# Second block's attention on one core: values of the latents a step later, copies ahead of splits, first sums ahead of a low part, no constant products

## What is computed

```
proj = rms_norm_2(x, attn_norm[l]) @ w_in[l]
h_mla, h_diff, h_ch = jnp.split(proj, [IN_MLA, IN_MLA + IN_DIFF], axis=-1)

# latents (MLA), 6 heads: queries and keys/values come out of small latents
q  = (rms_norm_2(c_q,  q_norm)  @ w_uq)
kv = (rms_norm_2(c_kv, kv_norm) @ w_ukv)
k_nope, v = kv[..., :MLA_NOPE], kv[..., MLA_NOPE:]

# differential, 6 heads, two score maps each; chunk, 4 heads with a relative bias
p = jax.nn.softmax(s, axis=-1)
o = einsum('bhqk,bkhd->bqhd', p, v)

x = x + jnp.concatenate([o_mla, o_diff, o_ch], axis=-1) @ w_out[l]
x = x + conv_ffn_2(rms_norm_2(x, ffn_norm[l]), w_ffn_in[l], ...)
```

## Time and profile before

| | us |
|---|---|
| median of 3 runs (1663.99 to 1665.25) | 1664.72 |
| profiled execution, its own time | 1663.76 |
| its span, from first to last instruction | 1662.5 |
| PE busy in the span | 1604.8 (97%) |
| DVE busy | 1045.5 (63%) |
| ACT busy | 804.7 (48%) |
| POOL busy | 238.1 (14%) |
| share of PE in the chain that ended last | 81% |
| mean granted TensorE clock | 0.993 |

### The profile page before, as it was taken

The page is one execution under the profiler, slowest core; times in us unless marked ns, Lnnn a source line. Parts: engine busy times, 40 slices in busy tenths (PEclk is TensorE's granted clock), DMA queues, the critical chain, the costliest instruction groups (busy, mean ns, idle before and its releaser), DMA issues.

```text
span 1662.5 us, 26953 instructions
## 1 busy us (share of the span) xinstructions
PE 1604.8 (97%) x10878; PEld 1387.7 (83%) x10878; DVE 1045.5 (63%) x1936; ACT 804.7 (48%) x1517; POOL 238.1 (14%) x284
## 2 busy tenths in 40 slices
PE   5999999999999999999999999999999999999998
PEld 3788778877777888887899988878999898799986
DVE  3553856366255435697787667656776667667765
ACT  2332963343233323568455544555555556555553
POOL 1110420011011000012011101132111013221110
PEclk9999999999999999999999999999999999999999
DMA  9557022353554224021445452424555533245552
GB/s 378 215 221 273 18 80 102 147 208 149 205 228 180 99 102 152 3 78 49 177 178 207 179 188 105 153 77 153 177 178 181 190 142 116 103 151 182 184 205 76
DMA packets 39419, 257.28 MB, mean 155 GB/s; under 512 B 5504, under 2 KB 6784, under 8 KB 10496
## 3 DMA queue, kind: packets, MB, share of 16 engines
q1 hardware_dynamic: 36416, 249.61, 41.1%
q0 software_dynamic: 1296, 4.72, 0.8%
q10 hardware_dynamic: 1584, 1.23, 0.3%
HBM read 254.49 MB, written 1.05 MB: 154 GB/s over the span
## 4 chain that ended last, share of the span: by engine, by line
PE 81%; DVE 10%; ACT 5%; DMA 2%; issue 2%; POOL 0%; SPq 0%; DVEq 0%; ACTq 0%
PE ps L485 24%; PE ps L487 24%; PE ps L486 24%; PE ps L501 2%; DVE wl L1758 1%; ACT arena L1665 1%; PE ps L632 1%; ACT wh L1317 1%; PE ps L654 1%; PE ps L641 1%; DVE ps L2017 1%; PE ps L527 1%; DMA arena<-in_xT 1%; PE ps L1066 1%; DMA raw<-in_ev_w_in 1%
## 5 line engine op out<-in xcount | busy, mean ns | idle before, releaser
L1758 DVE TENSOR_TENSOR wl<-raw,wh 128x1024 fp32r<-128x1024 f32 (+2 forms) x324 | 378.3, 1209 | 372.6 <-ACT wh L1317 372.0
L1317 ACT CAST wh<-raw 128x1024 fp32r<-128x1024 f32 (+2 forms) x334 | 328.7, 1034 | 515.7 <-PE ps L487 401.6
L485 PE MATMUL ps<-xh,wh 128*128 128x256 f32 (+1 forms) x1582 | 493.5, 312 | 3.0 <-ACT arena L1622 1.7
L487 PE MATMUL ps<-xh,wl 128*128 128x256 f32 (+1 forms) x1582 | 488.5, 309 | 0.0
L486 PE MATMUL ps<-xl,wh 128*128 128x256 f32 (+1 forms) x1582 | 488.5, 309 | 0.0
L485 PEld LDWEIGHTS ps<-xh,wh 128*128 128x128 f32 x1582 | 301.8, 191 | 28.1 <-issue 10.8
L486 PEld LDWEIGHTS ps<-xl,wh 128*128 128x128 f32 x1582 | 302.0, 191 | 15.2 <-issue 0.7
L487 PEld LDWEIGHTS ps<-xh,wl 128*128 128x128 f32 x1582 | 301.9, 191 | 15.2
L485 PE MATMUL ps<-wh,xh 128*128 128x512 f32 (+3 forms) x812 | 299.5, 369 | 13.9 <-DVE xl L2149 5.6
L487 PE MATMUL ps<-wh,xl 128*128 128x512 f32 (+3 forms) x812 | 294.6, 363 | 0.0
L486 PE MATMUL ps<-wl,xh 128*128 128x512 f32 (+3 forms) x812 | 294.6, 363 | 0.0
(11 more groups left out here) (212 smaller groups left out, 1840.9 us busy)
## 6 DMA issues: line engine op xcount, KB each, us to landing
raw<-in_ada SPq DMA_DIRECT2D x48, 1024.0 KB, 7.3
raw<-in_up SPq DMA_DIRECT2D x44, 1024.0 KB, 5.0
raw<-in_fin SPq DMA_DIRECT2D x44, 1024.0 KB, 4.8
raw<-in_down SPq DMA_DIRECT2D x22, 1024.0 KB, 4.8
raw<-in_fout SPq DMA_DIRECT2D x22, 1024.0 KB, 4.8
raw<-in_win SPq DMA_DIRECT2D x12, 1024.0 KB, 4.9
raw<-in_ev_w_in SPq DMA_DIRECT2D x9, 1024.0 KB, 8.0
raw<-in_wout SPq DMA_DIRECT2D x8, 1024.0 KB, 4.8
```

Of the source, the lines that this page charges most:

```text
L485: e.matmul(out, A[0], B[0], start=first, stop=False)
L487: return e.matmul(out, A[1], B[0], start=False, stop=last)
L1317: e.copy(hi_of(j)[:, a:b], raw_of(j)[:, a:b]).then_inc(*S.hi.up((j, half)))
L1758: e.tensor_tensor(lo_of(j)[:, a:b], raw_of(j)[:, a:b], hi_of(j)[:, a:b].bitcast(F), ALU.subtract).then_inc(*S.lo.up((j, half)))
```

## The change

It is made at eight places, the same in both layers:

1. PE: the two products for the latents' values leave `up_keys` (step 3) and become `up_values`, called in step 4 ahead of `column(7, 0)`. They go to banks 4 and 6 in place of 6 and 7.
2. PE: `keep(7, 2)`, `keep(b, 3)` and `keep(2, 5)` are taken out.
3. PE: `transposes` waits for the normalised probabilities first and for the bank second.
4. ACT and DVE: in step 2 the copies of the latents' queries stand ahead of the split of the `ukv` chunk.
5. ACT and DVE: the copies of the latents' values move from step 3 to step 4, ahead of the split of `win` 8, behind step 4's softmax work.
6. DVE: the low part of `wout` 1 moves from step 10 to step 11.
7. DVE: in step 13 `add_part("d", ...)`, the first sums, stands ahead of `mixed_low(10)`, the last low part.
8. `nb[0] = 0` restarts the turn of banks so that `column(7, 0)` still takes bank 7 and `column(7, 1)` bank 6.

```diff
@@ tensor_program
                     free[b] = [(side[g % 2], ("kn", l, g))]
-                for t, b in enumerate((6, 7)):
+
+            def up_values():
+                j = J[f"ukv{l}", 0]
+                hv, lv = hi_of(j), lo_of(j)
+                for t, b in enumerate((4, 6)):
                     wait_bank(b)
...
             def transposes(i):
                 for m in range(1 if i < 6 else 2):
                     b = 2 + (i % 2 if i < 6 else m)
+                    q.wait_ge(*(S.gps if m else S.vec).at((key, "norm", i)))
                     wait_bank(b)
-                    if i == 10 and m == 0:
-                        keep(b, 3)
-                    q.wait_ge(*(S.gps if m else S.vec).at((key, "norm", i)))
...
                     if i == 4:
-                        keep(7, 2)
+                        up_values()
+                        nb[0] = 0
                     column(7, i - 4)
...
-            keep(2, 5)
             for t in (1, 0):
                 out("m", t, [2], True, False, 1)
@@ scalar_program
             def beside(i):
-                if i == 3:
+                if i == 2:
+                    for g in range(3):
+                        copy2(("uq", l, g), QN[:, g, :], scale=qsc)
+                elif i == 3:
                     copy2(("kn", l, 0), KN[:, 0, :])
                     copy2(("kn", l, 2), KN[:, 2, :])
+                elif i == 4:
                     copy2(("vm", l, 0), VM[:, 0, :])
...
-                elif i == 2:
-                    for g in range(3):
-                        copy2(("uq", l, g), QN[:, g, :], scale=qsc)
@@ vector_program
-                if i == 3:
-                    copy2(("kn", l, 1), KN[:, 1, :])
-                    copy2(("vm", l, 1), VM[:, 1, :])
-                elif i == 10:
-                    turned_low(i)
-                if i in (1, 2, 3, 4, 10):
-                    weights(after({1: J[win, 5], 2: J[win, 6], 3: J[f"uq{l}", 0], 4: J[f"ukv{l}", 0], 10: J[win, 9]}[i]))
-                if i == 1:
-                    copy2(((win, 6), 1), VD[:, 1, :])
-                elif i == 2:
+                if i == 2:
                     q.wait_ge(*S.ea.at(("csq", l)))
...
+                elif i == 3:
+                    copy2(("kn", l, 1), KN[:, 1, :])
+                elif i == 4:
+                    copy2(("vm", l, 1), VM[:, 1, :])
+                elif i == 10:
+                    turned_low(i)
+                if i in (1, 2, 3, 4, 11):
+                    weights(after({1: J[win, 5], 2: J[win, 6], 3: J[f"uq{l}", 0], 4: J[f"ukv{l}", 0], 11: J[win, 9]}[i]))
+                if i == 1:
+                    copy2(((win, 6), 1), VD[:, 1, :])
...
-                if i == 13:
-                    add_part("d", 1)
-                    add_part("d", 0)
...
                 if 0 <= i - 1 < A.n:
                     normalise(i - 1)
+                if i == 13:
+                    add_part("d", 1)
+                    add_part("d", 0)
                 if i > A.lag:
                     mixed_low(i - A.lag - 1)
```

## The result

The changed kernel takes **1652.16 us** (median of 4 runs, 1651.02 to 1652.56); the kernel before took 1664.99 us beside it (4 runs, 1663.99 to 1665.42). The ratio is 0.9924, with an interval from 0.9912 to 0.9936: faster by 12.8 us. The profiled execution is the fastest of these four.

A forecast was written before the change was run, and what follows sets the result against it. It took PE's waits for releasers on DVE and ACT, not the constants, as the bound. Per layer 1.01 + 1.83 + 2.68 - 0.25 = 5.27 us, 10.5 for two, gave 1654.2 us, range 1652.4 to 1658.0.

The forecast's parts named there:

- three signs of being wrong: Pair 10's transposes still wait for DVE; `column(7, 0)` not at least 1 us earlier; a granted clock of 0.50 between them.
- Steps 2 to 4: Early attention loop: DVE's low part of `win` 7 comes 1.39 us earlier, leaving 1.01 us per layer at pair 4's transposes.
- The 0.37 us for the queries: Steps 2 and 3: PE gains 0.82 us from earlier query copies, of which only 0.37 us is left on DVE's chain.
- Steps 5 to 9: Middle of the loop: nothing touched up to step 10, so 1.0 us per layer is carried through.
- Pair 10 and part "m": Steps 10 to 13: pair 10's transposes start 1.83 us earlier, and part "m" gains 2.68 us more, per layer.
- `wout` 0: Behind part "m"'s start: PE waits for DVE's low part of this chunk; 0.25 us charged per layer, bounds 0 and 1.2.
- The sum: Both layers: 1.01 + 1.83 + 2.68 - 0.25 = 5.27 us per layer, 10.5 us in all.
- what a shifted phase may give in later stretches: Stretches after the loop: reason for extending the range's lower end from 1652.9 to 1652.4 us.
- The early part is real: Answers the rival that steps 2 to 4 give nothing, steps 10 to 13 keep 4.26 per layer: 1656.2 us, chance 0.13.
- The clock did not fall: Answers the rival of half-rate falls in the loop: at most 1.7 us each, one per layer gives 1657.6, chance 0.09.
- rival of the cheap constants: Pair 10 and part "m": DVE stays the bound, removed constants only become idle time; 1662 to 1665 us, chance 0.04.
- unseen releaser: Condition of the rival of the cheap constants: another engine's work holds pair 10's transposes and part "m" where they are.

The follow-up runs named there:

- number 1: Kernel before with only the three constant products that the change removes taken out; 1666.82 us beside 1664.40, ratio 1.0026.
- number 4: Changed kernel with `keep(b, 3)` ahead of pair 10's transposes and `keep(2, 5)` behind the loop put back; 1658.26 us beside 1664.22.
- number 2: Kernel before with only the late part of the change (1656.42 us, ratio 0.9954), or only the early part, steps 2 to 5 (1662.28 us, ratio 0.9986).
- number 5: Changed kernel, one edit undone each: splits ahead of queries' copies, 1653.23 us; wait order in `transposes`, 1652.79; low part of `wout` 1 in step 10, 1656.65.
- Numbers 5 and 6: 5 has its line under number 5; 6 is the changed kernel with part d's sums behind the last low part again, 1661.05 us beside 1664.17.
- number 7: Changed kernel with ACT splitting `wout` 0 ahead of its last-values work (1652.22 us, ratio 0.9928), or with `keep(7, 2)` back behind `up_values` (1653.32, 0.9933).

## Why the prediction was right, and where it was not

- **What bounds.** Right. The waits and not the constants set the loop: number 1 shows the constants worth nothing (or less) to remove alone, number 4 that 3.3 of 5.7 us are gone when the late ones stay. None of the three signs of being wrong that the prediction names was seen.
- **Steps 2 to 4.** Right by mechanism and size. 1.37 us was foreseen at the column and 1.51 found, 1.01 at pair 4 and 1.09 found; the waits of 0.6 to 0.8 and about 1.3 us came as 0.62 and 1.04; number 2 has the part alone at 1.11. The 0.37 us for the queries is the 0.4 of number 5.
- **Steps 5 to 9, "nothing from there to step 10 is touched".** The step of the sum that failed. Part 3, the order of the waits, was charged at nothing, without a reason. The gain grows from 1.09 to 1.32 us between pair 4 and pair 9, and by number 5 some 0.19 of these 0.23 us are that order. This is some 0.4 us in both layers, too little to put the time outside the range.
- **Pair 10 and part "m".** Right: 1.84 us for 1.83, 2.74 for 2.68. Numbers 5 and 6 undo one each and lose 1.9 and 2.6 us.
- **`wout` 0.** Right: 0.17 us by the ladder for the 0.25 charged, and 0.12 of it gone in number 7.
- **The sum.** 5.73 us a layer and not 5.27, so 11.4 us and not 10.5: 0.9 of the 2.0 us by which the median differs from the forecast. In a layer 0.23 us of the 0.46 came in steps 5 to 9 (0.15 to 0.19 of them the order of the waits), 0.08 is the early part, 0.06 part "m", 0.01 pair 10, and 0.08 the charge for `wout` 0, which was taken too high. With the measured 11.4 us in place of 10.5, the prediction's own reckoning gives 1653.3, inside its range.
- **The unchanged code, and the range.** This is the step that put the time outside. The prediction took the rest of the kernel over as it was in the median of the runs before (1664.72), and allowed 0.5 us below its best case, "for what a shifted phase may give in later stretches". The measured median is 1.1 us below the 1653.3. In the traces the difference lies ahead of the change and not behind it: 1.3 us of the spans' difference is there where nothing is changed, and the same program's runs span 5.9 us (1662.08 to 1667.94). The median of a new measurement can lie a good microsecond off for that reason alone, as 12.8 and 11.3 us for one and the same change show. Which side of the range's end the first four executions fell on was luck; that the range left no room for it was the mistake.
- **Rivals.** The early part is real (number 2). The clock did not fall in any loop of the changed kernel; numbers 1 and 6 show falls where the waits are longer, and a fall cost 0.8 to 1.5 us there, not more than the prediction's 1.7. Of the rival of the cheap constants one half was seen, that taken out alone they only turn into idle time (number 1); the unseen releaser that it needs is not there, since pair 10 and "m" came earlier once DVE's order had moved.

## What to carry to other kernels

Filler work in front of a wait costs nothing and is worth nothing to remove, until the releaser comes early; then it costs all of its pitch. So price the filler and the releaser's order as one edit: find what the releasing engine does ahead of the work that is waited for, and move that. Compare two executions from a mark just ahead of the changed place, and give the range of a forecast the spread of the unchanged code on either side.

## What the runs showed of the hardware

TensorE's clock fell in this loop only where constants were gone and the order was the old one at that place: behind the wait of 1.44 us in one of two loops (number 1), behind 2.60 us in three of four (numbers 1 and 6), behind 1.75 to 1.82 us in none of four (numbers 1 and 5), behind 1.04 to 1.08 us in none of eighteen. One fall cost 0.8 us where PE waits anyway soon after (pair 4 of number 1 at 35.47 for 34.67) and 1.1 to 1.5 us in the dense output projection (the end, behind "m", in numbers 6 and 1). Not expected at all was that the order of two waits on PE, both of which must be passed anyway, is worth 0.15 us a layer (number 5).
